# Full attention by pairs of heads: 64-column values in both halves of the array, weights summed by accumulating transfers

## What is computed

```python
def one_block(q_blk):
    s = jnp.einsum('bkgqd,bksd->bkgqs', q_blk, kt).astype(jnp.float32) * scale
    p = jax.nn.softmax(s, axis=-1).astype(vt.dtype)
    return jnp.einsum('bkgqs,bksd->bkgqd', p, vt)
```

## Time and profile before

| | |
|---|---|
| median of 3 runs | 1989.62 us (1987.11 to 1992.37) |
| the profiled execution | 1993.19 us, span 1991.4 us, mean granted clock of TensorE 0.994 |
| busy, share of the span | TensorE 97%, VectorE 61%, ScalarE 46%, GpSimd 5% |
| instructions | 23686 |

### The profile page before, as it was taken

One profiled execution on the slowest core, in us unless ns is written; L12 is line 12 of the kernel. 1 busy time (PEld: TensorE's weight loads), 2 busy tenths in 40 slices (PEclk: granted clock), 3 DMA queues, 4 the chain that ended last, 5 costly groups with the idle time before them and its releaser, 6 DMA issues.

```text
span 1991.4 us, 23686 instructions
## 1 busy us (share of the span) xinstructions
PE 1929.0 (97%) x8844; PEld 1507.2 (76%) x8844; DVE 1209.3 (61%) x1774; ACT 909.6 (46%) x1523; POOL 104.3 (5%) x188
## 2 busy tenths in 40 slices
PE   6999999999999989999999999999999999999898
PEld 4778876656787768888888788887888887776577
DVE  7795847655576787677555546656453555345744
ACT  6543345565553542332333434434523665455652
POOL 1101100000000000111000100000011000000000
PEclk9999999999999999999999999999999999999999
DMA  8426510010204423345111653333432000114052
GB/s 329 158 96 212 189 33 11 1 53 1 96 1 164 164 96 122 142 180 201 69 70 53 216 207 122 112 128 137 163 132 74 33 32 33 31 39 165 1 180 95
DMA packets 67151, 216.13 MB, mean 109 GB/s; under 512 B 8272, under 2 KB 13520, under 8 KB 66784
## 3 DMA queue, kind: packets, MB, share of 16 engines
q1 hardware_dynamic: 47168, 141.15, 20.1%
q0 software_dynamic: 19872, 73.48, 10.2%
HBM read 177.30 MB, written 34.61 MB: 106 GB/s over the span
## 4 chain that ended last, share of the span: by engine, by line
PE 85%; DVE 7%; ACT 3%; DMA 3%; issue 2%; SPq 0%; DVEq 0%; ACTq 0%
PE ps L1218 13%; PE ps L1220 13%; PE ps L1219 13%; PE ps L1368 9%; PE ps L1524 6%; PE ps L1525 6%; PE ps L1526 6%; PE ps L1344 3%; PE ps L1346 3%; DMA w_raw<-in_weights 2%; PE ps L1309 1%; DVE w_lo L2160 1%; PE ps L1312 1%; ACT w_hi L1691 1%; DMA ada_first<-in_ada 1%
## 5 line engine op out<-in xcount | busy, mean ns | idle before, releaser
L1218 PE MATMUL ps<-h_hi,w_hi 128*128 128x512 f32 x832 | 334.7, 402 | 9.7 <-DVE h_lo L2160 6.5
L1220 PE MATMUL ps<-h_hi,w_lo 128*128 128x512 f32 x832 | 325.9, 392 | 0.0
L1219 PE MATMUL ps<-h_lo,w_hi 128*128 128x512 f32 x832 | 325.4, 391 | 0.0
L2160 DVE TENSOR_TENSOR w_lo<-w_raw,w_hi 128x1024 fp32r<-128x1024 f32 x139 | 170.0, 1224 | 237.3 <-ACT w_hi L1691 235.7
L1691 ACT ACTIVATE w_hi<-w_raw 128x1024 fp32r<-128x1024 f32 x140 | 147.7, 1056 | 239.0 <-DMA w_raw<-in_weights 238.8
L2292 DVE TENSOR_REDUCE mh<-ps 128x1 f32<-128x512 f32 (+1 forms) x224 | 140.2, 630 | 143.9 <-PE ps L1309 67.9
L1218 PEld LDWEIGHTS ps<-h_hi,w_hi 128*128 128x128 f32 x832 | 157.9, 190 | 45.1 <-DVE h_lo L2160 7.7
L1220 PEld LDWEIGHTS ps<-h_hi,w_lo 128*128 128x128 f32 x832 | 156.9, 189 | 34.0
L1219 PEld LDWEIGHTS ps<-h_lo,w_hi 128*128 128x128 f32 x832 | 157.4, 189 | 32.1 <-issue 1.4
L1218 PE MATMUL ps<-hid_hi,w_hi 128*128 128x512 f32 x352 | 138.1, 392 | 3.9 <-DVE hid_kept_lo L2160 2.1
L1524 PE MATMUL ps<-t_hi,pair_S_r 128*128 128x512 f32 x352 | 137.2, 390 | 4.4 <-DVE pair_S_r L2160 2.6
(11 more groups left out here) (405 smaller groups left out, 3842.0 us busy)
## 6 DMA issues: line engine op xcount, KB each, us to landing
w_raw<-in_weights SPq DMA_DIRECT2D x140, 512.0 KB, 3.5
ada_next<-in_ada POOLq DMA_DIRECT2D x32, 512.0 KB, 4.7
ada_last<-in_ada POOLq DMA_DIRECT2D x24, 512.0 KB, 5.1
pair_gate<-in_weights SPq DMA_DIRECT2D x22, 512.0 KB, 3.5
pair_up<-in_weights SPq DMA_DIRECT2D x22, 512.0 KB, 4.5
ada_first<-in_ada SPq DMA_DIRECT2D x8, 1024.0 KB, 17.7
m_scratch<-y POOLq DMA_DIRECT2D x12, 512.0 KB, 5.9
hid_scratch<-hid_out POOLq DMA_DIRECT2D x22, 256.0 KB, 2.3
```

Of the source, the lines that this page charges most:

```text
L1218: e.matmul(o, w_hi[slot][:, tile_of(kw)], hi, start=start, stop=False, skip_group_check=skip)
L1219: e.matmul(o, w_hi[slot][:, tile_of(kw)], lo, start=False, stop=False, skip_group_check=skip)
L1220: return e.matmul(o, w_lo[slot][:, tile_of(kw)], hi, start=False, stop=stop, skip_group_check=skip)
L2160: return e.tensor_tensor(dst, src, hi.bitcast(F32), ALU.subtract)
```

## The change

The second and third attention kinds keep their order (`attention`); full attention gets its own, `paired`.

- **Order.** Two heads of the same queries, 2m and 2m+1, take turns unit by unit. Their maxima (16) are spread over the pair before. Value products are put down in groups of four units (`V_GROUP`), after the next scores, so a unit's product comes one to four units after its weights.
- **Values.** The stationary has 64 columns (values only). The even head writes rows 0 to 63 of the pair's bank, the odd head rows 64 to 127.
- **Denominators.** `psum` (`weight_sum`, on GpSimd): each unit's weights, 128 x 512, are copied (the first two units of a head) or added by an accumulating transfer into one of four sum tiles, two for each head. A link of such a chain waits for the one before it. `dsum` (`weight_sums`, on TensorE), three units after a pair's last: four products of 64 columns of ones with the four sums, into both halves of an auxiliary bank; `take` reads that bank in 128 rows, and `div` divides both heads at once. So 8 each of `dsum`, `take` and `div`.
- **Buffers.** Six weight buffers instead of three, four of queries and maxima instead of three, one of the inverses. The exponential of a unit waits for the value product and for the sum of the unit six before it.
- **Gate steps.** At units 3, 7, 11, 15, 30, 31, 46, 47, 62, 63, 78, 79, 80, 83, 86, 87, 88, 92, 95 instead of every fourth. The second key/value head is prepared at units 1 to 4. SP's second `back` also waits for the last sums.
- **Semaphores** are merged to make room (`kk_cp` and `kk_lo` into `kk_made`, four of the rotation into `qk_step`, `ln_r` into `inv`), with the counts to match. `mrow` of full attention takes its two halves by a reduction instead of a pairwise maximum.

The diff, cut to its core (blank lines left out too):

```diff
...
+    return [(kind, 2 * m + odd, n) for m in range(4) for n in range(2) for odd in range(2)]
...
+    maxima, rows, queries = {}, {}, {}
+    for m, start in enumerate(starts):
+        a, b = jobs[2 * m], jobs[2 * m + 1]
+        steps = [("max", *job, u) for job in (a, b) for u in max_units_of(*job)]
+        low, high = (starts[m - 1] + 1, start - 4) if m else (-4 - len(steps), -4)
+        at_g = [low + n * (high - low + 1) // len(steps) for n in range(len(steps))]
+        for g, step in zip(at_g, steps):
+            maxima.setdefault(g, []).append(step)
+        rows.setdefault(at_g[len(steps) // 2 - 1] + 2, []).append(("mrow", *a))
+        rows.setdefault(start - 2, []).append(("mrow", *b))
...
+    for g, (i, u) in enumerate(units):
+        job = jobs[i]
+        for step in at.get((job, u), ()):
+            p.add(*step)
+        if g + 1 < len(units):
+            p.add("sc", *jobs[units[g + 1][0]], units[g + 1][1])
+        for step in rows.get(g, []) + waiting + queries.get(g, []) + maxima.get(g, []):
+            p.add(*step)
+        waiting = [("div", *x[1:]) for x in waiting if x[0] == "take"]
+        p.add("psum", *job, u)
+        if g and g % V_GROUP == 0:
+            products(units[g - V_GROUP:g])
+        if i % 2 and g == last[i]:
+            ended.append((g + 3, job))
+        if ended and ended[0][0] == g:
+            p.add("dsum", *ended[0][1])
+            waiting.append(("take", *ended.pop(0)[1]))
+        other(share(job))
+    while fill:
+        for step in fill.pop(0):
+            p.add(*step)
+    products(units[len(units) - V_GROUP:])
+    for g, job in ended:
+        p.add("dsum", *job)
+        for kind in ("take", "div"):
+            p.add(kind, *job)
...
-    hook(0, 0, 1, *[x for i in sorted(beside) for x in beside[i]])
-    hook(2, 0, 2, ("attend", 1))
+    def unit(g, *steps):
+        pair, r = divmod(g, 2 * KT)
+        hook(2 * (pair // 2) + r % 2, pair % 2, r // 2, *steps)
+    unit(1, *[x for i in sorted(beside) for x in beside[i]])
     for half in range(2):
-        hook(2, 0, 4 + 2 * half, ("khi", "full", 1, half))
-        hook(2, 0, 5 + 2 * half, ("klo", "full", 1, half))
-    hook(3, 0, 2, ("vprep", "full", 1))
-    hook(5, 0, 0, ("back", 0))
-    for part in range(16):
-        i = 3 + 4 * part
-        hook(i // 16, i // 8 % 2, i % 8, ("gate", part))
-    for part, where in ((16, (5, 0, 2)), (17, (5, 0, 6)), (18, (5, 1, 2))):
-        hook(*where, ("gate", part))
+        unit(2 * half + 1, *([] if half else [("attend", 1), ("vprep", "full", 1)]), ("khi", "full", 1, half))
+        unit(2 * half + 2, ("klo", "full", 1, half))
...
-                self.v = [v_area[i](f"{n}_v{i}", [P, KT, P], F32) for i in range(2)]
+                self.v = [v_area[i](f"{n}_v{i}", [P, KT, 64 if n == "full" else P], F32) for i in range(2)]
...
-        A1 = Buffers("full", four(64, 72, 80, 88), four(68, 136), area, (76, 92, 144))
...
+        A1 = Buffers("full", four(64, 72, 80, 88), four(68, 136), area, (76, 92, 144, 94, 146, 78))
...
+        A1.qa.append(area("full_qa3", [P, HT], F32R))
+        A1.rinv = [Area(148, 150)("rinv1", [P, HT], F32)] * 2
+        A1.sums = [Area(start, start + 2)(f"p_sums{i}", [P, HT], F32) for i, start in enumerate((138, 150, 116, 118))]
...
+            if AUX[i][0] == "dsum":
+                return s["inv"], 2 * no(*AUX[i]) - 1
...
+                if kind == "full":
+                    e.matmul(ps[rows_of(h), bank, :], A.v[kb][:, u, :], weights[:, :], start=u == 0, stop=u == KT - 1,
+                             skip_group_check=True).then_inc(s["val"], 1)
+                    return
                 for kt, q0, q1, c in columns_of(kind, h, n, u):
                     o = ps[:, bank, q0 - n * HT:q1 - n * HT]
-                    x = e.matmul(o, A.v[kb][:, kt, :], A.pf[p3][:, c:c + q1 - q0], start=(u == 0 and kind != "band"), stop=False,
+                    x = e.matmul(o, A.v[kb][:, kt, :], weights[:, c:c + q1 - q0], start=(u == 0 and kind != "band"), stop=False,
                                  skip_group_check=True)
                 x.then_inc(s["val"], 1)
+            def weight_sums(kind, h, n):
+                bank = aux_bank("dsum", kind, h, n)
+                aux_free(("dsum", kind, h, n))
+                for part in range(2):
+                    for odd in range(2):
+                        e.wait_ge(*summed(kind, h - 1 + odd, n, KT - 2 + part))
+                        x = e.matmul(ps[rows_of(odd), bank, :], ones[:, 0:64], A1.sums[2 * odd + part][:, :], start=part == 0, stop=part == 1,
+                                     skip_group_check=True)
+                x.then_inc(s["den_mm"], 1)
...
             def scores(kind, h, n, u):
                 A, i = AB[kind], no("sc", kind, h, n, u)
                 c0, c1 = score_cols(kind, h, n, u)
-                p3, bank = (i - 1) % 3, 2 + i % 2
+                bank, weights = 2 + i % 2, weights_at(kind, i)
+                back = len(A.pf)
                 e.wait_ge(s["sc"], i)
-                if i > 3:
-                    e.wait_ge(s["val"], i - 3)
+                if i > back:
+                    e.wait_ge(s["val"], i - back)
+                    if kind == "full":
+                        e.wait_ge(*summed(*UNITS_IN_ORDER[i - back - 1]))
                 else:
                     e.wait_ge(s["m_kept"], kept(QM + 3, QM + 7, OM + 3))
-                e.activation(A.pf[p3][:, c0:c1], ps[:, bank, c0:c1], ACT.Exp, scale=SC).then_inc(s["p_exp"], 1)
...
-                e.wait_ge(s["val"], no("val", kind, h, n, last_unit((kind, h, n))))
-                if job >= 2:
-                    e.wait_ge(s["div"], job - 1)
-                e.activation(rinv[:, :], ps[64:P, bank, :], ACT.Ln).then_inc(s["ln_r"], 1)
-                e.wait_ge(s["ln_r"], job + 1)
+                if kind == "full":
+                    e.wait_ge(s["den_mm"], no("dsum", kind, h, n))
+                    if job >= 1:
+                        e.wait_ge(s["div"], job)
+                    e.activation(rinv[:, :], ps[:, aux_bank("dsum", kind, h, n), :], ACT.Ln).then_inc(s["inv"], 1)
+                else:
+                    e.wait_ge(s["val"], no("val", kind, h, n, last_unit((kind, h, n))))
+                    if job >= 2:
+                        e.wait_ge(s["div"], job - 1)
+                    e.activation(rinv[:, :], ps[64:P, bank, :], ACT.Ln).then_inc(s["inv"], 1)
+                e.wait_ge(s["inv"], 2 * job + 1)
                 e.activation(rinv[:, :], rinv[:, :], ACT.Exp, scale=-1.0).then_inc(s["inv"], 1)
...
             def divide(kind, h, n):
-                job = job_no(kind, h, n)
-                e.wait_ge(s["inv"], job + 1)
+                job = take_no(kind, h, n)
+                e.wait_ge(s["inv"], 2 * job + 2)
+                if kind == "full":
+                    e.wait_ge(s["val"], no("val", kind, h, n, KT - 1))
+                    tt(y[:, QA + h // 2, half_of(n)], ps[:, 6 + job % 2, :], A1.rinv[0][:, :], ALU.mult).then_inc(s["div"], 1)
+                    return
                 tt(q_src(kind, h, n), ps[0:64, 6 + job % 2, :], AB[kind].rinv[job % 2][:, :], ALU.mult).then_inc(s["div"], 1)
...
                     e.dma_start(z_dram[z_tiles.index(t)][:, half_of(n)], stage[c % 2][:, :]).then_inc(s["z_kept"], 16)
+            def weight_sum(kind, h, n, u):
+                pair, sums, (landed, count) = take_no(kind, h, n), A1.sums[chain_of(h, u)], summed(kind, h, n, u)
+                e.wait_ge(s["p_exp"], no("sc", kind, h, n, u))
+                src = weights_at(kind, no("sc", kind, h, n, u))
+                if u < 2:
+                    if pair:
+                        e.wait_ge(s["den_mm"], pair)
+                    elif h == 1:
+                        e.wait_ge(s["vt"], no("vprep", "full", 1))
+                    e.dma_start(sums[:, :], src[:, :]).then_inc(landed, 16)
+                else:
+                    e.wait_ge(landed, count - 16)
+                    e.dma_start(sums[:, :], src[:, :], accum_op=ALU.add).then_inc(landed, 16)
...
+                if part:
+                    for h in (last - 1, last):
+                        for u in (KT - 2, KT - 1):
+                            e.wait_ge(*summed("full", h, 1, u))
...
```

180 lines of the change are left out of this document (120 added, 60 removed).

## The result

The changed kernel takes 1997.98 us (median of 7 runs, 1996.27 to 2003.79), the kernel before 1990.09 us beside it (7 runs). The ratio is 1.0037, with an interval of 1.0023 to 1.0051: slower by 7 us, where 11 us faster was forecast. The profiled execution spans 1996.0 us, against 1991.4.

The account below looks back on a forecast made before the run. TensorE's stream was taken to bound full attention. The terms -41.3 + 17.2 + 8 + 5 - 2.5 + 3 sum to -10.6 us: 1979 us from a median of 1989.6, with a range taking in 1957 to 2014.

Parts of the forecast that it names:

- The bound, and the size of the stage's work: Full attention, 239 us: TensorE, busy for 235.9 us, sets the length; other engines have a third or more free.
- Values side by side, -41.3: Value products of two heads partly overlap, eight records in five steps of 0.43 us: 110.1 us become 68.8.
- Sums, +17.2: Denominators on TensorE: four value-like products for each of eight pair blocks, five steps each, 8 x 2.15 us.
- Changes of form, 80 x 0.1: TensorE enters and leaves the 64-column form 80 times at about 0.1 us each: +8 us, bounds 0 and 21.
- Rival D: Each change of form drains TensorE: +13 us on the sum, 1992 us; chance 0.09.
- Both fit, with less slack: Per group, VectorE's maxima (3.7 us) and ScalarE's exponentials (2.4 us) fit beside TensorE's 5.3 us: no cost.
- rival E: Bursts make VectorE and ScalarE late, two banks limiting TensorE's lead: 0.3 us a group, +10 us, 1989 us; chance 0.08.
- The aux bank held for the Ln, +5: Sum product's auxiliary bank stays taken until ScalarE's Ln reads it: TensorE waits 0.7 us for seven blocks, +5 us (0 to 10).
- The transfers, hidden: 128 transfers of 256 KB issued by GpSimd, 0.54 us each, stay hidden behind the stage's units: no cost.
- the condition: An accumulating transfer's unknown DMA price, at least 0.63 us, or 1.26; it would decide from 1.8 us on.
- The end, +3: After the last exponential, transfer (about 3 to 4 us) and sum product delay the first memory product: idle 4.6 us, before 1.7.
- rival B: Accumulating transfers become the stage's bound, exponentials waiting for landings: 2005 us taken, 2015 at four times a copy; chance 0.17.

Follow-up runs that it names:

- a control on the kernel before: The kernel before, with full attention's reductions reading 256 of 512 columns and the exponential's scale an eighth: 1991.94 us, ratio 0.9990.
- three edits that were meant to help: Each on the changed kernel: Ln, Exp and division right behind the sum product (2009.02 us); doubled maxima ahead of bursts, over 13 units (2015.10) or 12 (2009.82).

## Why the prediction was wrong

**The bound, and the size of the stage's work: right.** TensorE's stream is what counts, and its busy time fell by about as much as forecast.

**Values side by side, -41.3: mechanism right, size too small.** One premise failed here too, in the change's favour: "if TensorE starts records only in their order". The halves overlap wholly, four steps of 0.43. With changes of form, -39.7 came in place of -34.9. It is not more because each group took 0.13 us over the 2.07 of an undisturbed one (1.87, and 0.1 at each side); two bursts at half clock, 3.14 and 3.22 us long, are most of that, and waits on exponentials the rest. Rule and trace part here: the Trainium skill, "TensorE: Matmul & The Clock Gate", Part 3, has products start in program order, and with a0, a1, b0, b1 in the program the starts still came in pairs, in the same 1.87 us.

**Sums, +17.2: right in kind**, 15.9 with the changes of form where 18.8 was forecast, for the same reason.

**Changes of form, 80 x 0.1: too cheap.** 0.29 us in and out, so 40 x 0.29 = 11.6 us. The earlier trace rows showed the way in, and for the way out only its first part was read. Rival D had 21: the rows lie between. The Trainium skill, "TensorEngine Tiling (Array Packing)", Key Properties, says that changing the tiling mode drains the engine. If each change had let a product's last 0.16 us run out, in and out would have been 0.52 us where the trace has 0.29.

**"Both fit, with less slack": this is the step that failed, and without it the sign would not have turned.** The working compared VectorE's 3.7 us of maxima in a group with 5.3 us of TensorE's time, burst included. But a burst of value products hands VectorE nothing to reduce, and two banks carry two maxima over it; so the 3.7 us had to fit into the 3.1 to 3.8 us between bursts, with a division, copies and row reductions (1.9 us a group, as rival E said) besides. They did not. The waits of the stage came to 24.7 us for 2.5; cutting the reductions' length gave 11.5 us back, part of it clock, and the same cut gave the kernel before 2 or nothing. Not shown is how much of it is the bursts and how much the 16 maxima in 12 units. Some 5 us of it lie ahead of the first exponential, where sixteen maxima stand nearly alone; that the first pair has no earlier pair to hide its maxima under was nowhere in the prediction, and 3.6 us of it came back.

**The aux bank held for the Ln, +5: seen as forecast and worth little.** 6.2 us of waits, one before each of six pairs' maxima, but 1.4 us or nothing when removed. A wait that ends just before another one would have begun is not worth its length.

**The transfers, hidden: right inside the stage, and the condition held.** 1.28 us by their landings and 1.54 by their packets, under the 1.8 at which they would decide; the forecast had 1.26. GpSimd's 0.54 us for an issue was read from a plain store; an accumulating one took 0.84, still under a unit.

**The end, +3: mechanism right, too short by 3 us.** "About 3 to 4 us" for the last transfer was 7.0 (518.36 to 525.4): 2.7 of it until GpSimd, at 1.3 to 1.6 us from one issue to the next, reached the last, and 4.4 to land, behind others that landed 1.28 us apart. Here the transfers did set the time, as rival B had it for the whole stage.

**A term that the sum did not have: the clock.** 10 us of the stretch at 1.2 GHz, up to 5 us of time. For two thirds of it it comes with idle time and may be part of the same error; the rest has its like in a control on the kernel before.

What would have shown the result beforehand was there: rival E at 0.3 us a group gave 1989. At 0.7 us a group, which is what the 22.2 us of waits over the forecast's 2.5 are, it would have stood at 1979 + 22 = 2001.

## What to carry to other kernels

When work of one engine is gathered into bursts, compare the other engines' work with the time between the bursts, not with the whole period, and count what the buffers between them carry over. A tuned stream in which an engine with 60% load costs nothing can owe that to its even order; half the columns in the reductions were worth 2 us or nothing before and 11.5 after. A bound that sits close behind another gives no gain when the first is removed: price a removed wait by the next thing that is late. Behind a moved division, an Ln or a row turn look first at what is queued on the same engine; three edits that were meant to help cost 9 to 15 us that way.

## What the hardware showed

Not expected from the rows before:

- The two column halves of TensorE took their records independently: two-record fp32 products start 0.006 to 0.013 us apart whatever their order within the group.
- A change to the 64-column form and back cost 0.10 us in and 0.19 out, the latter spread over two products.
- An accumulating transfer of 256 KB inside SBUF occupied GpSimd for 0.84 us (a plain store 0.54), and the DMA engines for 1.54 us of packets (plain 0.70, by the rows of queue 0); with others waiting one landed every 1.28 us. It has twice the packets, 128 for 64 (16384 against 10240 in those rows). It landed in 4.2 us (the median with a quarter plain ones) where plain copies took 2.6.
- The DMA share reads 1.05 to 1.13 at 179 to 206 GB/s in these windows; in the earlier trace rows 1.03 went with 416: a full share says nothing of the bytes.
- The granted clock fell to 1.2 GHz inside a stage that had none of it: once behind 3.3 us in which TensorE was busy for 2.05, and once, at 461.3 us, behind 3.4 us in which it was busy throughout, 16 products of 8 columns among them. The second kind was in a control on the kernel before too, at 448.5 us.
